# One reduction and one weight remainder moved on VectorE, in the mixer of a two-layer decoder step

## What is computed

```
x = x + 0.5 * rms(swiglu(rms(x)))
x = x + rms(concat[A, B, C, D](rms(x) @ w_in) @ w_out)
x = x + 0.5 * rms(swiglu(rms(x)))
```

## Time and profile before

| what | value |
|---|---|
| three timed runs | 1413.53, 1413.85, 1406.39 us; median 1413.53 |
| the profiled execution | 1412.02 us, of which the span is 1410.2 us |
| TensorE matmul busy | 1280.8 us, 91% of the span |
| VectorE busy | 882.0 us, 63% |
| ScalarE busy | 625.6 us, 44% |
| GpSimd busy | 243.1 us, 17% |
| mean granted TensorE clock | 0.944 of full speed |

### The profile page before, as it was taken

One profiled execution on the slowest core, in us unless ns is written; L12 is line 12 of the kernel. 1 busy time (PEld: TensorE's weight loads), 2 busy tenths in 40 slices (PEclk: granted clock), 3 DMA queues, 4 the chain that ended last, 5 costly groups with the idle time before them and its releaser, 6 DMA issues.

```text
span 1410.2 us, 27848 instructions
## 1 busy us (share of the span) xinstructions
PE 1280.8 (91%) x9956; PEld 1196.1 (85%) x9956; DVE 882.0 (63%) x1490; ACT 625.6 (44%) x1175; POOL 243.1 (17%) x258
## 2 busy tenths in 40 slices
PE   6999999997868899999999999999877769999998
PEld 5999998996744689999989999999765439999996
DVE  3766546859755466664476664487786564766544
ACT  3665345446121354443465554553630225544343
POOL 2000012007555020000020000010466611100000
PEclk9999999999976799999999999999988769999999
DMA  7455555545586335555655555644346753455462
GB/s 241 150 182 182 148 166 159 189 149 113 158 237 201 120 120 182 183 174 152 191 168 179 179 162 164 199 157 156 92 153 201 218 173 120 145 183 178 141 185 92
DMA packets 286121, 234.17 MB, mean 166 GB/s; under 512 B 19898, under 2 KB 282018, under 8 KB 286056
## 3 DMA queue, kind: packets, MB, share of 16 engines
q1 hardware_dynamic: 281640, 229.44, 53.8%
q10 hardware_dynamic: 4416, 3.93, 1.0%
HBM read 228.65 MB, written 5.37 MB: 166 GB/s over the span
## 4 chain that ended last, share of the span: by engine, by line
PE 72%; DVE 12%; SPq 7%; issue 4%; DMA 2%; ACT 2%; DVEq 0%; POOL 0%; ACTq 0%; POOLq 0%
PE ps L1603 21%; PE ps L1604 21%; PE ps L1605 21%; SPq L470 2%; SPq L462 2%; DVE wlo L1061 2%; PE ps L1915 1%; DVE nlo L1115 1%; DVE s L1347 1%; DVE ps L1098 1%; PE ps L1963 1%; DMA raw<-in_w_in_dram 1%; ACT whi L611 1%; PE ps L1940 1%; PE ps L2022 1%
## 5 line engine op out<-in xcount | busy, mean ns | idle before, releaser
L1603 PE MATMUL ps<-nhi,whi 128*128 128x264 f32 x1936 | 559.8, 289 | 18.2 <-DVE wlo L1061 10.3
L1604 PE MATMUL ps<-nlo,whi 128*128 128x264 f32 x1936 | 552.6, 285 | 0.0
L1605 PE MATMUL ps<-nhi,wlo 128*128 128x264 f32 x1936 | 551.9, 285 | 0.0
L1061 DVE TENSOR_TENSOR wlo<-raw,whi 128x1024 fp32r<-128x1024 f32 (+2 forms) x364 | 380.6, 1087 | 267.2 <-ACT whi L611 266.7
L611 ACT ACTIVATE whi<-raw 128x1024 fp32r<-128x1024 f32 (+2 forms) x364 | 325.2, 943 | 160.9 <-PE ps L1605 108.5
L1603 PEld LDWEIGHTS ps<-nhi,whi 128*128 128x128 f32 x1936 | 368.6, 190 | 27.4 <-DVE nlo L1115 14.2
L1604 PEld LDWEIGHTS ps<-nlo,whi 128*128 128x128 f32 x1936 | 369.0, 191 | 0.2
L1605 PEld LDWEIGHTS ps<-nhi,wlo 128*128 128x128 f32 x1936 | 367.1, 190 | 0.0
L1603 PE MATMUL ps<-hhi,whi 128*128 128x264 f32 x704 | 203.0, 288 | 9.1 <-DVE hlo L1083 9.1
L1605 PE MATMUL ps<-hhi,wlo 128*128 128x264 f32 x704 | 202.1, 287 | 0.0
L1604 PE MATMUL ps<-hlo,whi 128*128 128x264 f32 x704 | 201.9, 287 | 0.0
(11 more groups left out here) (350 smaller groups left out, 1416.8 us busy)
## 6 DMA issues: line engine op xcount, KB each, us to landing
raw<-in_ffn_gate_dram SPq DMA_DIRECT2D x44, 1024.0 KB, 5.4
raw<-in_ffn_up_dram SPq DMA_DIRECT2D x44, 1024.0 KB, 5.3
raw<-in_ffn_down_dram SPq DMA_DIRECT2D x64, 704.0 KB, 4.5
raw<-in_w_in_dram SPq DMA_DIRECT2D x24, 1024.0 KB, 5.7
kslot<-in_cache_fox_k_dram SPq DMA_DIRECT2D x128, 128.0 KB, 2.9
vslot<-in_cache_fox_v_dram SPq DMA_DIRECT2D x128, 128.0 KB, 4.0
raw<-in_w_out_dram SPq DMA_DIRECT2D x8, 1024.0 KB, 5.2
kslot<-in_state_swa_k_dram SPq DMA_DIRECT2D x32, 128.0 KB, 3.0
```

Of the source, the lines that this page charges most:

```text
L1061: tt2(wlo[s][:, a:b], raw[s][:, a:b], whi[s][:, a:b].bitcast(F32), ALU.subtract).then_inc(S(f"w_lo{s}"), 1)
L1603: mm(out, wh, hi_, start=first, stop=False)
L1604: mm(out, wh, lo_, start=False, stop=False)
L1605: return mm(out, wl, hi_, start=False, stop=last)
```

## The change

The eighth `sample_add` is moved from behind `sample_out(2)` to the end of the last level, behind `state_new`. The low part of w_out's first block in slot 0 is moved from behind the last squares to the place ahead of `sample_out(3)`. No instruction is added or removed, on any engine.

```diff
-                               3: [...], 4: [...], 5: [state_new]}
+                               3: [...], 4: [...], 5: [state_new, lambda: sample_add(7)]}
...
                     sample_out(2)
-                    sample_add(7)
                     dve.wait_ge(S("vn_mm"), V("vn_mm", 2))
                     dve.tensor_copy(vn[:, 1, :], ps[:, 0, 0:GW]).then_inc(S("vn"), 1)
...
                     smp_square(512, 768)
+                    lo("wo", 0, 0)
                     sample_out(3)
                     dve.wait_ge(S("mix_r"), V("mix_r", 6))
...
                     smp_square(0, 512)
-                    lo("wo", 0, 0)
                     dve.wait_ge(S("mix_r"), V("mix_r", 7))
                     smp_scale(0, 512)
```

More of the change, by code:

```diff
@@ L1478, in _ @@
                     between = {0: [lambda: sample_top(0), conv_scale], 1: [lambda: add(3), gmlp_norm], 2: [lambda: sample_top(1), lambda: add(4), gmlp_mix],
-                               3: [lambda: state_sum(0)], 4: [lambda: sample_top(2), lambda: add(6), state_value], 5: [state_new]}
+                               3: [lambda: state_sum(0)], 4: [lambda: sample_top(2), lambda: add(6), state_value], 5: [state_new, lambda: sample_add(7)]}
                     for k, b in enumerate(LEVELS):
```

## The result

| | before | after |
|---|---|---|
| median, 16 runs each | 1413.34 us (1406.39 to 1419.81) | 1402.90 us (1398.45 to 1407.89) |
| the profiled execution | 1412.02 us, span 1410.2 | 1401.42 us, span 1399.6 |
| mean granted clock, profiled | 0.944 | 0.948 |

The ratio is 0.9929, with a 95% interval from 0.9913 to 0.9946: the change makes the kernel 10.0 us faster (7.6 to 12.3). The forecast was 1406.0, a gain of about 7. The sign and the range hold. The sum of 6.8 us falls short by 3.2 and lies just outside the interval.

A forecast was written before the change was run, and what follows sets the result against it. Bound: the mixers' chain of engines taking turns, both moved pieces on it. First layer 3.3 us, second 3.6, less 0.1: 6.8 saved, giving 1405.2 from the profiled execution, 1406.7 from the median; forecast 1406.0, range 1400 to 1411.5.

The forecast's parts named there:

- the clock: At w_out's transposes and product, a rise 3 us sooner or later per layer: up to 3 us in all, either way.
- Rival 3: The granted clock takes the new order better or worse: 1403 or 1409; chance 0.24, half to each side.
- Part 1, the saving at the second copy: Second copy of `vn` starts sooner, waiting next for `new_values(1)`: 2.02 us saved in the first layer, 2.03 in the second.
- Part 1, the room in the new place: Moved reductions fit VectorE's idle time before the first copy of `vn`, with 0.46 us to spare, 1.27 in the second layer.
- Rival 2: The moved reductions and GpSimd's products hold each other: 3.0 us lost, about 1409; chance 0.04.
- The 0.3 us at line 1359: First layer: the samples' bias is held by GpSimd's last product; 0.3 us lost, bounds 0 and 0.6.
- The reductions beside GpSimd: In their new place GpSimd's products slow the reductions by nothing; other bound: held for 2.36 us.
- Part 2: Low part of w_out moved into VectorE's idle time before line 1387: line 1550 starts 1.58 us sooner in each layer.
- Slot 1's load: w_out's load moves up about 2 us, just in time for ScalarE's conversion; back-to-back loads cost 0.1 us over both layers.
- rival 1: Slot 1's load doesn't move up and ScalarE stands before line 874: 2 to 3 us lost, about 1408.5; chance 0.14.
- Rival 5: Slower: w_out's first load is late, so the moved subtractions hold VectorE before `sample_out(3)`; 1420; chance 0.03.
- Rival 4: TensorE's last pair doesn't wait for the copy of `vn`: only 3.2 us saved, 1409.5; chance 0.04.

The follow-up runs named there:

- e4: The changed kernel with the eighth sample's second reduction moved behind st_s: 1401.05 us, ratio 0.9946 to the kernel before.
- e7: The changed kernel with slot 0's second load of w_out held back until the samples' scale is done: 1399.76 us, ratio 0.9910.
- e1: The kernel before with only the eighth sum moved, the subtractions left in their old place: 1406.45 us against 1409.3, ratio 0.9989.
- e2: The kernel before with only the two subtractions (low part of w_out) moved: 1402.81 us, ratio 0.9945.
- e3: The changed kernel with 30 unused matmuls in TensorE's stop ahead of w_out's transposes: 1394.73 us, ratio 0.9891 to the kernel before.
- e6: The kernel before with 43 unused matmuls in TensorE's stop ahead of w_out's transposes: 1403.40 us, ratio 0.9926.
- e9: e6 (old order) with 14 more unused matmuls ahead of the down product of both feed-forward passes: median 1394.49 us, ratio 0.9891.
- e11: e8 with the eighth sum back in its old place, the subtractions still moved: median 1392.45 us, ratio 0.9869 to the kernel before.
- e10: The same kernel as e8, run again in one series with e9 and e11: median 1390.60 us, ratio 0.9860 to the kernel before.
- e8: e3 with 14 more unused matmuls ahead of the down product of both feed-forward passes: 1389.62 us, ratio 0.9834 to the kernel before.

## Why the prediction was right, and where it fell short

**The term that was mis-sized is the clock.** The prediction wrote a rise "3 us sooner or later", "either way", and put 0 into the sum. The gain measured without fillers is 10.0 us, with fillers 5.2: the clock adds about 4.8, with an uncertainty of some 3.6. The two come from different series, and the gain without fillers moves between series by about as much: the nearly equal e4 and e7 gave 7.6 and 12.7 us by their ratios. In the series of e1 and e2 part 2 alone took 11.7 us off the time at 1.2 GHz (159.3 to 147.6). Between the single traces of the kernel before and of e2 three places make 10.2 us: 3.6 in the stops themselves, in which nothing is lost, 3.2 in transposes and product, and 3.4 behind the stop near 641 us. The last two are worth 3.3 us at half speed, and e2's gain lies 3.8 (by means) to 4.6 us above its price of 3.2. In the stage it is shown by e3 and e6 that the excess is the clock's; for the kernel as a whole e9 to e11 agree, within their uncertainty. The time at 1.2 GHz of the kernel before itself differs between series (159.3, 161.6 and 168.2 us). Rival 3's good half, 1403, was the right case, but in part by luck: the rise came 2.3 and 0.8 us sooner relative to the product and not 3 in each layer, and the rest lay behind the stop near 641 us, where the prediction had not looked. Why a stop shorter by 1.6 us goes with an earlier rise, and why the dip near 641 us is tied to part 2 although its own stop has the same length in both kernels (2.08 and 2.07 us), stays open; each trace is one execution.

**Part 1, the saving at the second copy.** Right in size and reason: 1.74 and 2.07 us, not 3.05, because the copy waits for `new_values(1)` next. The first layer missed 0.3 us of its 2.02 because line 1508 took 0.82 us beside a GpSimd product instead of 0.53.

**Part 1, the room in the new place.** Wrong for the first layer, and the largest error but the clock. The 0.46 us to spare came from one execution's idle time. In it `new_values(0)` ended 4.75 us after line 1473 began; in the changed kernel's 2.87 us after (432.61 - 429.74). Line 1473 itself kept its distance from the landing of the values that starts TensorE's work, 3.0 us in both. What changed is how fast TensorE got through the `sample_values` ahead of `new_values(0)`. Its 28 matmuls in the chain of the kernel before, with the clock at 1.2 GHz until 432.76, and on TensorE's timeline of the changed kernel, with the clock at 2.4 GHz from 424.92:

```profile
428.71 3.59 PE ps L1915 x28
```

```profile
426.78 1.91 PE L1914 MATMUL ps<-vslot,s 128*4 128x257 f32 x28 [1.58 <-DMA vslot<-in_cache_fox_v_dram]
```

From their start to the end of `new_values(0)` it was 7.76 us before and 5.83 after, and these 1.93 us are the whole loss of room. The idle time that the prediction spent was largely the slow clock of one execution.

Six profiled kernels have both reductions in the new place (the changed one, e1, e3, e7, e8, e10). In three of their twelve places the first copy was held, all in the first layer, by 1.35, 0.64 (e3) and 1.45 us (e10). There the way from `new_values(0)` to the second copy took 9.3 to 10.2 us; in the other nine it took 7.2 to 8.8, and in the ten places of the kernels with the old order (before, e2, e6, e9, e11) 9.5 to 10.8. So where the copy is held nearly the whole gain of part 1 in that layer is gone. In the profiled execution it nets 2.08 - 0.42 = 1.7 us, and 1.9 by e11 and e10, not 3.7. Rival 2 gave a loss of 1.9 us in the first layer; a loss of 1.35 us and what follows from it came by another mechanism.

**The 0.3 us at line 1359** did not occur in the changed kernel's execution. Its GpSimd timeline:

```profile
441.71 1.25 POOL L1023 TENSOR_TENSOR tok<-tok,og 128x512 f32<-128x512 f32 x1
```

It ended at 442.96, 2.1 us sooner than before, so the bias at 442.88 met only its end and took 0.21 us. But this is because the first copy was held. Counted from the start of line 1473, GpSimd ended after 13.2 us, as before (13.3), and the bias began after 13.1 us, where the prediction had it at 12.6. In e1 and e8, where the first copy was not held in this layer, it began after 12.6 us and the collision took place. VectorE's and GpSimd's timelines of e8:

```profile
443.42 0.85 DVE L1359 SCALAR_TENSOR_TENSOR s<-s,bias 128x64 f32<-128x64 f32 x1
```

```profile
442.93 1.25 POOL L1023 TENSOR_TENSOR tok<-tok,og 128x512 f32<-128x512 f32 x1
```

The bias took 0.84 to 0.87 us in four of the twelve places (e1 and e8 in the first layer, e8 and e10 in the second, for which the prediction had put nothing), 0.64 longer than alone. From the second copy to `spread_max(3)` it is then 4.4 us, where it is 3.94 in the kernel before and 3.96 in the changed one. So the loss is 0.45 us where it occurs, within the bounds of 0 and 0.6.

**The reductions beside GpSimd** were priced at nothing, and that held. The sixteen reductions of the changed kernel, against the earlier trace rows:

```profile
L1347 DVE TENSOR_REDUCE s<-kslot x16: 2267/2278/2287, 337.8 to 1114.3; 128x32 f32<-128x2048 f32 x16
```

The eighth's first one ran beside two GpSimd products (431.11 to 434.87) in 2.28 us. By the rule of the Trainium skill that the prediction weighed (SBUF — State Buffer, "Who interferes with whom") reductions take no part in the port lock and two-input instructions do; the traces agree with both halves, 2.28 us here, and line 1508 at 0.42 to 1.44 us and line 1359 at 0.21 to 0.87 us over the runs.

**Part 2.** Right: from the start of the last squares' reduction to the scale it was 2.87 us (464.36 to 467.23) and is 1.28 (460.45 to 461.73), 1.59 less. Of the 1.28 us, 0.60 are the wait for ScalarE, and 0.51 us are left before line 874. The subtractions took 2.34 us in the idle time and nothing waited for them. e3 against e6 gives 1.6 us a layer, e11 against e9 3.3 us in all.

**Slot 1's load** was in time, so rival 1 fell. SyncE's issues in the changed kernel, against the earlier trace rows, and the times to landing of the two loads issued there:

```profile
440.21 0.40 SPq L366 DMA_DIRECT2D raw<-in_w_out_dram  x1
...
455.81 1.05 SPq L366 DMA_DIRECT2D raw<-in_w_out_dram  x2
```

```profile
DMA to landing us min/median/max: 5.2/6.4/7.7
```

Slot 1's load, issued first, took 5.2 us and landed at about 461.0, so that ScalarE's conversion of slot 1 began at 461.60 right behind line 870; it was just in time, as the prediction said. The 7.7 us are slot 0's second load, issued 0.5 us behind it, which is not needed so soon. The 5.9 us of the earlier trace rows, by which the prediction priced such a pair, belong to a load whose successor was issued 2.6 us later, so the row was no measure of it. In rival 1 line 874 would have come at 466.3 by the sum itself, not at 465.9, so its first loss was 0.8 us and not 1.2. e7, which keeps them apart, is no slower and not surely faster. Rival 5 fell as well: w_out's first load was issued at 440.21 and its high part was ready before the subtractions at 452.90. Rival 4 fell with the first row of the stretches.

## What to carry to other kernels

When a change shortens a stop of TensorE in front of a dense product, price the clock as a gain with a sign and not as symmetric noise, and measure the order with the stops filled if its own worth is wanted. Idle time of one engine in one trace is room only as long as the work that ends it takes as long again: look at the clock under which that work ran, and reckon with half its time before spending 85% of the room. Price a collision from the distance between the two instructions, and expect that distance to change with every other delay on the way: here the collision took place just where the first copy was not held.

## What the runs showed of the hardware

- Stops of 2.1 to 2.4 us are enough to bring the granted clock down to 1.2 GHz for 3.4 us behind 21 of 36 of them, and not behind others that look alike; with unused matmuls in them, behind none of 16. Matmuls into an unused bank during these stops and the one before the w_out product are worth 15.4 us on the old order (e9, 0.9891), and with the change the gain is 20 to 23 us (e10, e8).
- With the clock held, a tile's transposes start every 0.52 us, at 1.2 GHz every 0.82, and the matmuls of the product every 0.12 against 0.22 us.
- The same two-input VectorE instruction of 128x256 (line 1508) took from 0.42 to 1.44 us, by how it met GpSimd's products; the one of 128x64 (line 1359) took 0.21 us alone and 0.85 when a product of GpSimd had begun 0.5 us before it, and ended with that product.
- Two 1 MB loads issued 0.5 us apart landed after 5.2 and 7.7 us, where others in this stage took 5.0 to 5.5; the single one issued at 440.21, right behind sixteen loads of values, took 7.3.
